# Ten cache copies in rows of 10 KB in place of 5: one decoder step on one core

## The reference, cut to what matters

```
proj = x @ w_in                       # 1024 -> 4096: q, k, v, gate, and four parts for a short convolution
o    = dilated window attention(q, keys, values)      # 8 heads of 64, three windows
att  = o * silu(g_att);   z = gb * conv3(gc * hh) * silu(g_conv)
y    = LayerNorm(alpha * x + concat(att, z) @ w_out)
new_k, new_v = the last 2048 rows of concat(cache, new)   # for each of the 8 sequences
```

## Time and profile before

| | us |
|---|---|
| median of 3 runs (lowest, highest) | 352.95 (352.83, 353.74) |
| the profiled execution's own time | 351.81 |
| its span, first to last instruction | 349.8 |
| TensorE busy | 340.7 |
| DMA, mean over the span | 402 GB/s, 140.52 MB |
| ScalarE's queue / SyncE's queue | 64.23 MB / 75.83 MB |

### The profile page before, as it was taken

How to read it: one execution, slowest core, us unless ns; L and a number is a source line. 1 busy time by engine, 2 the same in 40 slices (tenths; PEclk the granted TensorE clock), 3 DMA queues, 4 the chain that set the end, 5 groups by cost and what they waited for, 6 DMA issues and landing times.

```text
span 349.8 us, 7201 instructions
## 1 busy us (share of the span) xinstructions
PE 340.7 (97%) x2984; PEld 298.1 (85%) x2984; DVE 210.1 (60%) x406; ACT 123.8 (35%) x257; POOL 16.4 (5%) x40
## 2 busy tenths in 40 slices
PE   8999999999999999999999999999999999999991
PEld 6998988997989889979898899798879887888791
DVE  3745528955254657652546586525546699894884
ACT  5624424342244423423443334234453744400100
POOL 0130000000200000002000000020000001100000
PEclk9999999999999999999999999999999999999998
DMA  7999999999999999999999999999999999999995
GB/s 294 393 417 416 419 421 419 421 423 418 420 406 422 423 418 420 381 418 418 414 419 423 420 413 383 421 399 399 427 421 418 416 419 350 388 386 395 403 359 227
DMA packets 31714, 140.52 MB, mean 402 GB/s; under 512 B 3137, under 2 KB 3905, under 8 KB 26689
## 3 DMA queue, kind: packets, MB, share of 16 engines
q1 hardware_dynamic: 16034, 75.83, 53.3%
q10 hardware_dynamic: 15648, 64.23, 46.5%
HBM read 132.15 MB, written 71.86 MB: 583 GB/s over the span
## 4 chain that ended last, share of the span: by engine, by line
PE 94%; DVE 3%; ACT 1%; issue 0%; DVEq 0%; ACTq 0%
PE pj_b L1334 11%; PE pj_b L1336 10%; PE pj_b L1335 10%; PE pj_a L1334 9%; PE pj_a L1335 8%; PE pj_a L1336 8%; PE sc L1497 5%; PE sc L1530 4%; PE px L1682 3%; PE px L1684 3%; PE px L1683 3%; PE po L1477 3%; PE px L1445 3%; PE pt L1463 3%; DVE rg L1038 1%; PE sc L1362 1%
## 5 line engine op out<-in xcount | busy, mean ns | idle before, releaser
L1334 PE MATMUL pj_b<-x_hi,w_hi 128*128 128x320 f32 x248 | 78.5, 316 | 0.3 <-DVE mix L1054 0.3
L1335 PE MATMUL pj_b<-x_lo,w_hi 128*128 128x320 f32 x248 | 76.5, 308 | 0.0
L1336 PE MATMUL pj_b<-x_hi,w_lo 128*128 128x320 f32 x248 | 76.5, 308 | 0.0
L1334 PE MATMUL pj_a<-x_hi,w_hi 128*128 128x256 f32 (+1 forms) x248 | 71.3, 288 | 0.0
L1335 PE MATMUL pj_a<-x_lo,w_hi 128*128 128x256 f32 (+1 forms) x248 | 69.5, 280 | 0.0
L1336 PE MATMUL pj_a<-x_hi,w_lo 128*128 128x256 f32 (+1 forms) x248 | 69.5, 280 | 0.0
L909 DVE TENSOR_TENSOR w_lo<-w_raw,w_hi 128x1024 fp32r<-128x1024 f32 x30 | 37.1, 1235 | 26.8 <-ACT w_hi L573 26.8
L1334 PEld LDWEIGHTS pj_a<-x_hi,w_hi 128*128 128x128 f32 x248 | 46.8, 189 | 5.5 <-issue 3.7
L1334 PEld LDWEIGHTS pj_b<-x_hi,w_hi 128*128 128x128 f32 x248 | 46.5, 188 | 4.9 <-issue 3.6
L1336 PEld LDWEIGHTS pj_a<-x_hi,w_lo 128*128 128x128 f32 x248 | 46.7, 188 | 0.0
L1335 PEld LDWEIGHTS pj_a<-x_lo,w_hi 128*128 128x128 f32 x248 | 46.6, 188 | 0.0
(11 more groups left out here) (189 smaller groups left out, 477.1 us busy)
## 6 DMA issues: line engine op xcount, KB each, us to landing
k_buf<-in_k_used SPq DMA_DIRECT2D x16, 1280.0 KB, 12.3
v_buf<-in_v_used SPq DMA_DIRECT2D x20, 1024.0 KB, 14.5
out_k_used_out<-in_k_used ACTq DMA_DIRECT2D x16, 1280.0 KB, 17.7
out_v_used_out<-in_v_used ACTq DMA_DIRECT2D x17, 1024.0 KB, 16.2
w_raw<-in_w_tiles SPq DMA_DIRECT2D x30, 512.0 KB, 8.9
out_k_rest_out<-in_k_rest ACTq DMA_DIRECT2D x12, 1024.0 KB, 13.8
out_v_rest_out<-in_v_rest ACTq DMA_DIRECT2D x12, 1024.0 KB, 13.9
wo_raw<-in_w_out SPq DMA_DIRECT2D x8, 512.0 KB, 17.8
```

Of the source, the lines that this page charges most:

```text
L1334: nc.tensor.matmul(out, w_hi[:, w], x_hi[:, c], start=(k == 0), stop=False)
L1335: nc.tensor.matmul(out, w_hi[:, w], x_lo[:, c], start=False, stop=False)
L1336: return nc.tensor.matmul(out, w_lo[:, w], x_hi[:, c], start=False, stop=(k == KT - 1))
```

## The change

The copies of keys are numbered 0 to 15 in the order of their issue. From number 6 on, a copy takes the rows as they are, 10 KB each, 8 of them for each DMA engine, in place of 16 of 5 KB. The bytes, the place of the issue and the engines stay.

```
+LONG_FROM = 6
...
             def copy_k(i, c):
                 rows = slice((K_PIECES * i + c) * P, (K_PIECES * i + c + 1) * P)
+                if K_PIECES * i + c >= LONG_FROM:
+                    out, keys = (d[name][rows, :].rearrange("(r a) n -> a r n", a=16) for name in ("k_used_out", "k_used"))
+                    act.dma_start(out, keys).then_inc(copied, 16)
+                    return
                 act.dma_start(short_runs(d["k_used_out"][rows, :]), short_runs(d["k_used"][rows, :]))\
                     .then_inc(copied, 16)
```

## The result

The changed kernel takes 356.16 us (median of 6, 355.58 to 358.22) against 353.0 for the kernel before in the same runs: ratio 1.0105, 95% interval 1.0076 to 1.0134. It is 1.1% slower by the ratio, some 3.7 us, and 3.2 by the medians, where 2.0 were forecast. The profiled execution is the longest of the six, 358.22 us, with a span of 356.2; 1.7 us of that were lost ahead of the last stage (tile 0's first use of `x_res` starts at 307.51, before at 305.81). No long row can have caused it: ScalarE's issue of a copy at 290.2 is already 1.7 late, and the first row of 10 KB starts at 293.4.

A forecast was written before the change was run, and what follows sets the result against it. TensorE, busy 340.7 of 349.8 us, was taken to bound the kernel up to the last product. A late tile 1 store (+3.0) less the end gain (-1.0) on 352.95 gave 354.9 us, eight in ten 352.0 to 357.6.

The forecast's parts named there:

- The share of the queues: DMA engines take one row from each queue in turn, so 10 KB rows double ScalarE's bytes per row of SyncE's.
- Rival C: DMA engines share by whole copies, 80 KB whatever the row; landings stay, 352.9 us; chance 0.10.
- The bytes ahead of tile 1's store: From 297 to that store's end both queues move 16.65 MB, 5.5 MB of it SyncE's.
- the landing of that store: Tile 1's store on SyncE's queue lands at 340.3 us instead of 330.8; ends 339.2 to 341.6.
- The rate: Both queues together move 410 GB/s, so the 16.65 MB take 40.6 us.
- The start: Long rows flow from about 296, and the rows of tile 0's x_res begin at 297 as before.
- The wait of VectorE and its slack: VectorE starts the last tile 4.1 us late; less 1.13 us of slack, 3.0 us on the path.
- The covers: Other late SyncE transfers, x_res of tiles 2 and 4 and tile 0's store, cost nothing.
- The end gain: The last two store halves meet empty queues and take 2.6 us: 1.0 us gained, bounds 0 to 1.3.
- The sum: Profiled 351.81 + 3.0 - 1.0 = 353.8 us; the same 2.0 on the median gives 354.9 us.
- Rival B: Tile 1's store lands before 337.3, in time, and the end gains 1.0 to 1.3 us: 351.8; chance 0.22.
- Rival D: Long rows run at 375 GB/s or less; store lands at 344 or later, +5.8 us, 358.7; chance 0.10.

The follow-up runs named there:

- f4: The changed kernel itself, ten copies of keys with 10 KB rows, timed once more against the kernel before: ratio 1.0085.
- e4: The changed kernel with rows of 2.5 KB, 32 for each engine, in the last ten copies of keys: 356.03 us, ratio 1.0044 to the kernel before.
- e3: The kernel before, no long rows, with tile 4's result put in x_res: ratio 0.9986 to the kernel before.
- e1: The changed kernel with tile 4's result in x_res, so VectorE doesn't wait for tile 1's store: 352.68 us, ratio 0.9938 to the kernel before.
- f1: The changed kernel with 10 KB rows in the last two copies of keys only: ratio 0.9994 to the kernel before.
- f2: The changed kernel with 10 KB rows in the last four copies of keys only: ratio 0.9983 to the kernel before.
- g2: The changed kernel with tile 4's result in x_res and 10 KB rows in seven copies (9 to 15): ratio 0.9991 to the kernel before.
- g3: The kernel before with tile 4's result in x_res and store_values viewed as 4 KB rows, which went out as 8 KB: ratio 0.9996.

## Why the prediction was right, and where it was off

**The share of the queues: right.** 386 packets to 400 after, 1233 to 1240 in f4. ScalarE's queue gets nearly twice the bytes for each row of SyncE's. Rival C, share by whole copies, is out: in e4 a copy has 32 rows an engine and a load 8, and the packets are 330 to 332. Equal counts alone would also come of bundles of the same number of rows from either queue. The starts and lengths of the packets settle that: in f4, from 300 to 340, 899 of SyncE's 1009 rows end within 4 ns of the start of one of ScalarE's, where starts that happen to fall there would make some 225, and 251 of one of SyncE's own, where some 213 would. Where both queues have work, a row is a turn. The Trainium skill ("DMA: Bandwidth & Descriptors", "Queues, rings and completion order") has packets of typically 9 to 17 descriptors there; these traces don't agree, and the measurement decides.

**The bytes ahead of tile 1's store: right.** 16.65 MB were worked out, 5.5 of them SyncE's; f4 has 16.79 and 5.51 between 299 and 342.

**The step that was mis-sized: the landing of that store, 340.3 forecast, 345.4 in f4,** whose last stage begins 0.4 later than in the profile before; 4.7 us too early. Three parts. The rate: 391 GB/s in f4, not 410, is 42.6 us for 16.65 MB in place of 40.6, 2.0 us; I had weighed the loads of rows 8 too much and the copies' own 397 too little. The start: I let the long rows begin at 296 and the rows of `x_res` at 297 as before. But copy 5 lands when its slowest engine is done, and the first row of 10 KB starts at 292.8 in f4. So the rows ahead of `x_res` are held back too, among them the 8 short ones an engine of `new_conv` (288 bytes each), which take their turns like any other: in f4, from 294 to 300, 106 of 127 end within 4 ns of the start of one of ScalarE's rows, where chance would make 36. Its time to landing in f4:

```profile
DMA to landing us min/median/max: 10.4/10.4/10.4
```

Before it is 7.9, and 8.6 in e3, so `new_conv` is some 2 us later; `x_res` of tile 0 lands at 305.8 in f4 against 301.7, 3.7 late beyond the 0.4, where 8 rows of 5 KB more would be 1.6. About 2 us lie there. Some 0.7 is left, which no run explains.

**The wait of VectorE and its slack: right.** In f4 the last tile starts at 345.50, 8.9 us later than 336.19 + 0.4, and the halves are issued at 353.1 and 353.7, 7.6 us later than 345.1 + 0.4 and 345.75 + 0.4. The difference, 1.3, is the slack of 1.13 and 0.2 more. The covers held: VectorE waited 3.9 us for `x_res` of tile 2, and it cost nothing. The store of tile 0 came out at 328.9, and cost 0.4 us of a wait that I had put at none.

**The end gain: right in kind, too small.** The halves land in 2.0 and 2.1 us in the changed kernel. I counted 1.0 us from 3.6 to 2.6. Against an ordinary run it is from 4.6 to 2.1, 2.5 us. I had read the size of the collision from the shortest run there was. The path to it was wrong in one point: I had the last copy land by 344 to 346, and it lands at 349.2 in f4, hardly earlier than in e3 (349.6). The queues are empty for the halves because the halves are 7 us later, not because the copies are earlier.

**The sum.** Forecast +3.0 - 1.0. In the traces, against e3, whose span is 351.3: the halves are issued 7.4 us later (353.7 to 346.3) and land 2.5 sooner, 4.9 on the path, for a difference of spans of 5.0. By the ratios it is less, +3.0 to +3.7, and by the medians +3.2 and +3.9; the profiled runs of the changed kernel are at the top of their range (358.2 and 358.3). So each of the two terms came out at two and a half times its forecast, with opposite signs; that the sum was 1 to 2 us off and no more is in part luck. By ratios, taking the slot wait away is worth 1.0085 - 0.9938 or 1.5%, 5.2 us, and what is left of the change is a gain of 0.6%, 2.2 us (0.5% against e3). That gain is not the 2.5 us above: in e1 the last half takes 3.9 us, and the last copy lands at 348.3. (By its own sum the likeliest range of the prediction ends at 357.7, not 357.4: 390 GB/s puts the landing at 342.4.)

**Rival B, in time:** its gain exists, and e1 shows it whole, but the point at which it decides, a landing before 337.3, was missed by 8 us. **Rival D, a lower rate:** the rate of 391 lies between its 375 and my 410. Its landing, 344 or later, is the one that came, outside the 339.2 to 341.6 of the forecast, but of the 4.7 us by which the landing was off only 2.0 are the rate; its price of +5.8 did not come, as the end gave back more.

**Where the gain comes from** is not fully settled. What f1 and f2 exclude is the rate of the long rows by themselves. What the table suggests is that SyncE's rows last longer beside long ones, so that ScalarE's queue is alone for less time: 350 to 362 GB/s from 330 to 342 with up to four long copies, 387 to 407 with seven or ten. Over that window g2 doesn't fit, with 387 GB/s and no gain in time. Over the whole stage, from 299 to 342, it does: 391 to 394 GB/s with ten long copies, 384 with seven in g2, 376 to 381 with up to four (387 in the short profile before), 369 in e4. That is an order of the sizes and no proof; no run changes the time that ScalarE's queue is alone and nothing else. g3 was meant to, and did not do what it should.

## What to carry to other kernels

When two queues share the DMA engines row by row, a longer row on one is a longer wait for each row of the other, however short that is. Add up what stands in the slowed queue ahead of each transfer that somebody waits for, row by row with one of the other queue's beside each, and look for waits on a store's landing as well as on loads: here it was a buffer slot, 5.4 us ahead of its use, that broke, and moving one tile's result elsewhere turned a loss of 1% into a gain of 0.5 to 0.6%. And read the size of a collision from several executions; one profile can be the lucky one.

## What the runs showed of the hardware

Where both queues had work, the DMA engines took one row from each in turn, with 2.5 KB (332 packets of SyncE's to 330), 5 KB (599 to 601) and 10 KB (1240 to 1233) on ScalarE's side and 4 or 8 KB on SyncE's.

Copies from memory to memory alone in their queue ran at some 334 GB/s with rows of 2.5 KB, 348 and 355 with 5 KB and 328 to 358 with 10 KB, against 380 to 420 where a second queue worked beside them; a single queue of such copies left about a tenth of the rate unused whatever the row.

A DMA newly issued on SyncE's queue, with nothing of its own ahead, started its first row only 3.6 to 4.0 us later while ScalarE's queue was full of copies (e4, issued at 312.2 and first row at 315.8; before, 336.3 and 340.3). It was 0.8 with ScalarE's queue empty (f4, 353.1 and 353.9), and also at 345.1 in the profile before, where ScalarE's last copy was nearly done.

And the issue of a DMA with 512 rows, 578 ns when the queue was short, could hold ScalarE for up to 8.5 us when it was long (e4), with other work of the engine waiting behind.
